# Eight-head mixer of a transformer kernel: values for two query tiles side by side with the values stationary, probabilities normalised on GpSimd, and no turn of the outputs

## The chip, the cores and the metric

One core of a Trainium2 chip runs the whole program. Its engines are TensorE (PE), VectorE (DVE), ScalarE (ACT), GpSimd (POOL) and SyncE (SP), each with its own instruction queue that it works off in order; they wait for each other by semaphores. The metric is the device time of one execution in microseconds, median of several runs.

## What is computed

Two transformer blocks, one after the other, on 512 tokens of width 1024, in float32. The stage that the change touches is the first half of the first block. It has two attention mixers over the same normalised input: an indexed one (called A1 in the kernel), whose keys for each query are the 128 with the best index score, and a latent one (B1) with eight heads of 64 and causal attention. In the latent mixer, per head and per block of 128 queries:

```
sc = (q_nope . k_nope + q_rope . k_rope) * scale
sc = where(causal, sc, -inf)
p  = softmax(sc)
o  = p @ v            # 128 queries x 64, for each of eight heads
...
y_b = o_b @ w_branch_b          # 512 -> 1024
merged = sigmoid(g_a) * y_a + sigmoid(g_b) * y_b
```

In the index part each of four query tiles needs its 128 largest of 512 scores. The kernel takes them in 16 rounds of eight.

## The kernel before

Every dense product is made of three matmuls per 128x128 weight tile: weights and inputs are split into a high and a low half (`w_hi`, `w_lo`, and the same for the inputs), and high times high, high times low and low times high are added up. ScalarE writes `w_hi` (L1710) and VectorE writes `w_lo` (L2272) for each set of weights, into one of two slots; TensorE may start an item when the first half of its tiles is split, and the split for the item after next comes when the item is done.

The stage is written out by hand as one list, `FRONT_ORDER`, which all engines walk, each doing its own part of each entry. `work_of_front` makes it. A unit is one head and one query tile: units 0 to 31 are the latent mixer (head u//4, tile u%4), units 32 to 63 the indexed one. For each unit v a slot of entries is laid down by `slot(v)`:

- `turn v+1`: TensorE transposes the 128x512 probabilities of unit v+1 (L1286), ScalarE copies them to `pt` (L1790), and then does the exponentials (L1781) that were asked for since the last turn;
- `score v+4`: TensorE makes the scores (L1250), VectorE adds the mask and takes the maximum (L2354 to L2360);
- `value v`: TensorE multiplies the turned probabilities with the values (L1296), ScalarE scales the result by one over the row sum and writes it to `front_rows` (L1801);
- `top`: one or two rounds of the largest-eight search, on VectorE alone (L2259 and L2260; at the end of a tile also L2262, L2263 and L2257);
- at the end of every second head `oturn`: TensorE transposes the 512x128 outputs of two heads (L1329), ScalarE and VectorE write their high and low halves (L1817, L2376).

At the start of a head there is `vturn`, which transposes its values. Between these entries, in each place that the list marks `None`, tiles of dense work are spread evenly: per head the item `bkv` (1 tile), `bq` (2 tiles) and a gate (8 tiles), and for the last two heads 24 tiles of the indexed mixer's projections. After a `bq` comes `rope`: a matmul (L1237), a multiplication on GpSimd (L1115) and two additions on VectorE (L2340, L2344). The split of the next weights (`later`) is issued by ScalarE and VectorE at the next `turn`, `vturn`, `oturn`, `value` or `both`.

Units from 32 on already work as the change makes the others work: GpSimd normalises the probabilities of two units before they are turned (L1123), and one `both` makes the values of two units with the values stationary and the probabilities moving (L1309). ScalarE and VectorE write the high and low halves of the result straight from the accumulator (L1823, L2382). VectorE inverts the row sums (L2369) of units j+1 and j+2 at `turn j`, for odd j, and waits there for the exponentials of unit j+2. For units below 32 it inverts unit j at `turn j`.

After the list, the branch products, the output projection, the feed-forward layers and the second block follow, most of the time; the change does not touch them.

Of the kernel before, what the change touches and what calls it, by code (L numbers as in the profile page):

```python
# [23 lines left out]
P = 128  # L24
D = 1024
SEQ = 512
META = 16
T = META + SEQ
# [150 lines left out]
def work_of_front():  # L179
# [23 lines left out]
    def slot(v):  # L203

        if v >= 32:
            p, e = (v - 32) // 2, [("vturn", 9)] if v == 32 else []
            if v % 2:
                e += [("both", p), None] + ([("turn", v + 1), None] if v + 1 < FRONT_VALUES else [])
# [10 lines left out]
        e += [("value", v), None]  # L219
        if v % 8 == 7:  # L220
            e += [("oturn", v // 8), None]
# [101 lines left out]
def front_outputs(v):  # L323

    return v + 1 if v < 32 else 32 + (v - 32) // 2 + 1
# [211 lines left out]
def events(phase):  # L537
# [5 lines left out]
    if kind == "front":  # L543
        e = items(len(FRONT_ITEMS[0::2]), len(FRONT_ITEMS[1::2]))
        units, ropes = FRONT_VALUES, len(ROPES)
        e.update(s_full=48, scored=units, negm=units, probs=units, rinv=units, o_full=48, o_out=48,
                 o_hi=16, normal=32, pt_full=len(FRONT_TURNED), pt_a=len(FRONT_TURNED), o_low=4, turned=ropes, roped=ropes, rope_step=ropes,
# [101 lines left out]
def build(nc, A, out):  # L649
    with ExitStack() as ctx:  # L650
# [226 lines left out]
        def front_output(k):  # L877

            return [x[:, k, META:T] for x in outputs["B1"]], turned_of

        def front_pair(p):

            i, t, _ = front_unit(32 + 2 * p)
            at, o = META + P * (t - 1), P * (1 + p % 2)
            return [x[:, i, at:at + P] for x in outputs["A1"]], acc[:, 3, o:o + P]
# [177 lines left out]
        def _(pool):  # L1063
# [10 lines left out]
            for index, ph in enumerate(PHASES):  # L1074
# [29 lines left out]
                if ph == ("front",):  # L1104

                    for what, j, *part in FRONT_ORDER:
# [13 lines left out]
                        elif what == "turn" and j >= 31 and j % 2 and j + 2 < FRONT_VALUES:  # L1120
                            for u in (j + 1, j + 2):
# [31 lines left out]
        def _(pe):  # L1153
# [39 lines left out]
            def front():  # L1193

                def dense(j, first, end):
# [3 lines left out]
                    if first == 0:  # L1199
# [4 lines left out]
                        if kind == "branch":  # L1204
                            if name == "B1":
                                pe.wait_ge(S["o_low"], n.at("o_low", 4))
                            else:
                                pe.wait_ge(S["o_out"], n.at("o_out", 48))
# [57 lines left out]
                def bank_free(x):  # L1266
# [4 lines left out]
                    else:  # L1271
                        pe.wait_ge(S["pt_a"], n.at("pt_a", x - 1))
                        kind, k = FRONT_TURN_LIST[x - 2]
                        if kind == "oturn":
                            pe.wait_ge(S["o_low"], n.at("o_low", k + 1))

                def turn_probs(v):

                    x = FRONT_TURNED["turn", v]
                    if v < 32:  # L1280
                        pe.wait_ge(S["probs"], n.at("probs", v + 1))
                    else:
                        pe.wait_ge(S["normal"], n.at("normal", v - 31))
# [6 lines left out]
                def values(v):  # L1290

                    made = FRONT_TURNED["vturn", front_unit(v)[0]]
                    pe.wait_ge(S["pt_a"], n.at("pt_a", max(FRONT_TURNED["turn", v], made) + 1))
                    pe.wait_ge(S["o_out"], n.at("o_out", v))
                    for b in range(4):
                        mm = pe.matmul(acc[:, 3, 64 * (v % 2):64 * (v % 2) + 64], pt[:, v % 2, 1 + b, :],  # L1296
                                       front_values(v)[:, 1 + b, 0:64], start=b == 0, stop=b == 3)
                    mm.then_inc(S["o_full"], 1)

                def values_of_pair(p):  # L1300

                    u = 32 + 2 * p
                    made = FRONT_TURNED["vturn", 8 + front_unit(u)[0] // 2]
                    pe.wait_ge(S["pt_a"], n.at("pt_a", max(FRONT_TURNED["turn", u + 1], made) + 1))
                    pe.wait_ge(S["o_out"], n.at("o_out", 32 + p))
# [7 lines left out]
                def turn_values(k):  # L1313
# [7 lines left out]
                    mm.then_inc(S["pt_full"], 1)  # L1321

                def turn_outputs(k):

                    pe.wait_ge(S["o_out"], n.at("o_out", 8 * k + 8))
                    x = FRONT_TURNED["oturn", k]
                    bank_free(x)
                    for b in range(4):
                        mm = pe.transpose(turned_of[x % 2][:, b * P:(b + 1) * P], front_rows[:, b, :], eye)  # L1329
                    mm.then_inc(S["pt_full"], 1)  # L1330
# [84 lines left out]
                for what, j, *part in FRONT_ORDER:  # L1415
# [24 lines left out]
                    elif what == "value":  # L1440
                        values(j)
                    elif what == "both":
                        values_of_pair(j)
                    elif what == "vturn":
                        turn_values(j)
                    elif what == "oturn":
                        turn_outputs(j)
# [254 lines left out]
        def _(act):  # L1702
# [30 lines left out]
            def front(following):  # L1733
# [59 lines left out]
                def take_output(v):  # L1793

                    at, t, _ = front_unit(v)
                    row, d = t - 1, 64 * (at % 2)
                    act.wait_ge(S["o_full"], n.at("o_full", v + 1))
                    act.wait_ge(S["rinv"], n.at("rinv", v + 1))
                    if v % 8 == 0 and v:
                        act.wait_ge(S["pt_full"], n.at("pt_full", FRONT_TURNED["oturn", v // 8 - 1] + 1))  # L1800
                    act.activation(front_rows[:, row, d:d + 64], acc[:, 3, 64 * (v % 2):64 * (v % 2) + 64], ACT.Identity,  # L1801
                                   scale=rinv8[:, v % 8:v % 8 + 1]).then_inc(S["o_out"], 1)

# [8 lines left out]
                def take_outputs(k):  # L1812

                    x = FRONT_TURNED["oturn", k]
                    (hi, _), bank = front_output(k)
                    act.wait_ge(S["pt_full"], n.at("pt_full", x + 1))
                    act.activation(hi, bank[x % 2], ACT.Copy).then_inc(S["pt_a"], 1)  # L1817
# [77 lines left out]
                for what, j, *part in FRONT_ORDER:  # L1895
# [41 lines left out]
                    elif what == "value":  # L1937
                        take_output(j)
# [4 lines left out]
                    elif what == "oturn":  # L1943
                        take_outputs(j)
# [265 lines left out]
        def _(dve):  # L2210
# [96 lines left out]
            def front(following):  # L2307
# [54 lines left out]
                def invert(v):  # L2362

                    dve.wait_ge(S["probs"], n.at("probs", v + 1))
                    if v >= 40:
                        dve.wait_ge(S["normal"], n.at("normal", v - 39))
                    elif v >= 8:
                        dve.wait_ge(S["o_out"], n.at("o_out", v - 7))
                    dve.reciprocal(rinv8[:, v % 8:v % 8 + 1], rowsum8[:, v % 8:v % 8 + 1]).then_inc(S["rinv"], 1)  # L2369

                def take_low(k):

                    x = FRONT_TURNED["oturn", k]
                    (hi, lo), bank = front_output(k)
                    dve.wait_ge(S["pt_a"], n.at("pt_a", x + 1))
                    dve.tensor_tensor(lo, bank[x % 2], hi.bitcast(F32), ALU.subtract).then_inc(S["o_low"], 1)  # L2376

                def take_both(p):

                    (hi, lo), bank = front_pair(p)  # L2380
                    dve.wait_ge(S["o_hi"], n.at("o_hi", p + 1))
                    dve.tensor_tensor(lo, bank, hi.bitcast(F32), ALU.subtract).then_inc(S["o_out"], 1)  # L2382
# [101 lines left out]
                for what, j, *part in FRONT_ORDER:  # L2484
# [420 lines left out]
```

## Time and profile before

| | |
|---|---|
| median of 3 runs | 2276.22 us (2275.92 to 2276.91) |
| the profiled execution | 2279.35 us, span 2277.5 us |
| granted TensorE clock, mean | 0.995 |
| TensorE busy | 2219.2 us (97%) |
| VectorE busy | 1243.9 us (55%) |
| ScalarE busy | 903.5 us (40%) |
| GpSimd busy | 220.5 us (10%) |
| eight heads of the latent mixer | about 130 to 300 us |

Busy time is that of recorded instructions; matmuls overlap each other in the records, so that TensorE can show as busy in a stretch in which it had short waits.

### The profile page before, as it was taken

The numbers are of one execution on the slowest core, as the hardware profiler recorded it, in microseconds if no ns is written. First come the engines' busy times: TensorE is split into PE (matmuls) and PEld (weight loads), VectorE is DVE, ScalarE is ACT, GpSimd is POOL, SyncE is SP. The second block draws the span as 40 slices with busy tenths as digits, with TensorE's granted clock in tenths as the row PEclk, the third lists the DMA queues.
The fourth block names the chain that finished last, engine by engine and source line by source line (L and its number), as shares of the span: only waits on it lengthen the run. The fifth ranks groups of instructions, "written<-read, shape, count | busy, mean of one in ns | idle before, by whom it ended". The sixth has DMA issues, their size and how long they took to land.

```text
span 2277.5 us, 36049 instructions
## 1 busy us (share of the span) xinstructions
PE 2219.2 (97%) x12592; PEld 1820.2 (80%) x12592; DVE 1243.9 (55%) x2668; ACT 903.5 (40%) x1815; POOL 220.5 (10%) x201
## 2 busy tenths in 40 slices
PE   8999999999999999999999899999999999999998
PEld 6567766778888889999999777777777787888887
DVE  5779786467736745533442545544555655443442
ACT  5455445444414443322322444444444433322332
POOL 0100043310000031000001000111100130000001
PEclk9999999999999999999999999999999999999999
DMA  4111211235533342342233222243333233332332
GB/s 119 36 37 37 65 47 52 79 102 150 157 102 95 113 129 78 91 129 88 85 106 99 57 85 81 74 111 94 98 92 98 81 97 89 95 108 77 97 105 75
DMA packets 400393, 205.67 MB, mean 90 GB/s; under 512 B 68956, under 2 KB 393928, under 8 KB 400284
## 3 DMA queue, kind: packets, MB, share of 16 engines
q1 hardware_dynamic: 399365, 203.83, 31.3%
q8 instruction: 63, 1.03, 0.2%
q10 hardware_dynamic: 919, 0.43, 0.1%
q14 instruction: 46, 0.38, 0.1%
HBM read 201.94 MB, written 14.80 MB: 95 GB/s over the span
## 4 chain that ended last, share of the span: by engine, by line
PE 64%; issue 19%; DVE 4%; ACT 2%; POOL 1%; POOLq 0%; DVEq 0%; ACTq 0%
PE acc L1169 34%; PE acc L1474 16%; PE acc L1220 5%; PE sco L1509 2%; PE acc L1573 1%; PE acc L1569 1%; DVE w_lo L2272 1%; PE sco L1262 1%; PE sco L1549 1%; POOL vT L1095 1%; PE acc L1309 1%; PE acc L1549 0%; PE sco L1529 0%; PE acc L1296 0%; DVE bias L2260 0%
## 5 line engine op out<-in xcount | busy, mean ns | idle before, releaser
L1710 ACT ACTIVATE w_hi<-raw 128x512 fp32r<-128x512 f32 (+4 forms) x656 | 372.0, 614 | 694.4 <-PE acc L1169 661.2
L2272 DVE TENSOR_TENSOR w_lo<-raw,w_hi 128x512 fp32r<-128x512 f32 (+4 forms) x656 | 423.2, 685 | 143.8 <-ACT w_hi L1710 139.5
L1169 PE MATMUL acc<-xn_hi,w_hi 128*128 128x512 f32 (+1 forms) x1408 | 421.1, 340 | 2.1 <-DVE qbuf L2826 2.1
L1169 PE MATMUL acc<-xn_lo,w_hi 128*128 128x512 f32 (+1 forms) x1408 | 422.1, 340 | 0.0
L1169 PE MATMUL acc<-xn_hi,w_lo 128*128 128x512 f32 (+1 forms) x1408 | 420.3, 339 | 0.0
L1169 PEld LDWEIGHTS acc<-xn_hi,w_hi 128*128 128x128 f32 x1408 | 241.9, 188 | 35.8 <-DVE qbuf L2826 3.0
L1169 PEld LDWEIGHTS acc<-xn_lo,w_hi 128*128 128x128 f32 x1408 | 241.2, 188 | 31.2 <-issue 0.5
L1169 PEld LDWEIGHTS acc<-xn_hi,w_lo 128*128 128x128 f32 x1408 | 241.5, 188 | 30.0
L1169 PE MATMUL acc<-hid_lo,w_hi 128*128 128x512 f32 (+1 forms) x832 | 261.5, 349 | 0.0
L1169 PE MATMUL acc<-hid_hi,w_lo 128*128 128x512 f32 (+1 forms) x832 | 260.6, 348 | 0.0
L1169 PE MATMUL acc<-hid_hi,w_hi 128*128 128x512 f32 (+1 forms) x832 | 259.8, 347 | 0.8 <-DVE hid_lo L2768 0.8
L2826 DVE TENSOR_TENSOR qbuf<-acc,v_tok 128x512 f32<-128x512 f32 (+1 forms) x132 | 91.7, 695 | 249.8 <-PE acc L1169 249.7
L1474 PE MATMUL acc<-xn_hi,w_hi 128*128 128x264 f32 (+1 forms) x576 | 187.7, 367 | 13.2 <-DVE xn_lo L2299 3.8
L2778 DVE SCALAR_TENSOR_TENSOR h<-acc,h 128x512 f32 (+3 forms) x64 | 44.5, 695 | 267.6 <-PE acc L1169 267.6
L1474 PE MATMUL acc<-xn_hi,w_lo 128*128 128x264 f32 (+1 forms) x576 | 172.8, 341 | 0.0
L1474 PE MATMUL acc<-xn_lo,w_hi 128*128 128x264 f32 (+1 forms) x576 | 172.5, 340 | 0.0
L1169 PEld LDWEIGHTS acc<-hid_hi,w_hi 128*128 128x128 f32 x832 | 144.5, 188 | 23.2 <-issue 1.1
L1169 PEld LDWEIGHTS acc<-hid_lo,w_hi 128*128 128x128 f32 x832 | 144.5, 188 | 21.2
L1169 PEld LDWEIGHTS acc<-hid_hi,w_lo 128*128 128x128 f32 x832 | 144.8, 188 | 20.4
L1474 PEld LDWEIGHTS acc<-xn_hi,w_hi 128*128 128x128 f32 x576 | 98.7, 189 | 36.8 <-issue 17.8
L1220 PE MATMUL acc<-xn_hi,w_hi 128*128 128x512 f32 x240 | 118.6, 494 | 0.9 <-DVE w_lo L2272 0.6
L1474 PEld LDWEIGHTS acc<-xn_hi,w_lo 128*128 128x128 f32 x576 | 99.3, 189 | 12.6
(397 smaller groups left out, 3065.7 us busy)
## 6 DMA issues: line engine op xcount, KB each, us to landing
raw<-in_w_ffn_in SPq DMA_DIRECT2D x176, 256.0 KB, 3.0
raw<-in_w_in SPq DMA_DIRECT2D x118, 256.0 KB, 3.2
raw<-in_w_up SPq DMA_DIRECT2D x88, 256.0 KB, 3.0
raw<-in_w_ffn_out SPq DMA_DIRECT2D x32, 384.0 KB, 3.3
raw<-in_w_gate SPq DMA_DIRECT2D x48, 256.0 KB, 3.0
raw<-in_w_ffn_out SPq DMA_DIRECT2D x32, 320.0 KB, 3.7
raw<-in_w_out SPq DMA_DIRECT2D x32, 256.0 KB, 2.8
bias<-grids_dram SPq DMA_DIRECT2D x64, 128.0 KB, 2.9
```

The lines of the kernel that those rows point to most:

```text
L1095: ins = pool.tensor_tensor(square_sum[:, c0:T], square_sum[:, c0:T], probs[:, s, c0:T], ALU.add)
L1169: mm = pe.matmul(acc[0:m, 2 * slot + b, 0:size], w[slot][:, t, 0:m], x[:, place(t), c:c + size], start=(t == 0 and w is w_hi and x is xh), ...
L1220: mm = pe.matmul(acc[0:m, slot, 0:SEQ], w[slot][:, t, 0:m], x[:, t, META:T], start=(t == 0 and w is w_hi and x is xh), stop=(t == tiles - ...
L1262: mm = pe.matmul(sco[:, hh, :], queries_a[i][r, P * (t - 1):P * t], kbuf[r, i // 2, META:T], start=True, stop=True)
L1309: mm = pe.matmul(acc[64 * hh:64 * hh + 64, 3, o:o + P], front_values(u)[:, 1 + b, 0:64], pt[:, hh, 1 + b, :], start=b == 0, stop=b == 3)
L1474: mm = pe.matmul(acc[:, b if wide else slot, 0:size], w[slot][:, t, :], x[:, t, c:c + size], start=(t == 0 and w is w_hi and x is xh), sto ...
L1509: mm = pe.matmul(sco[:, bank, to:to + size], qbuf[r, i % 2, TILES[t][0]:TILES[t][0] + P], kbuf[r, keys_at(name, i), c:c + size], start=Tru ...
L1549: mm = pe.transpose(turned_of[x % 2][:, b * P:(b + 1) * P], prob_of[u % 4][:, real + b * P:real + (b + 1) * P], eye)
L1710: act.activation(w_hi[slot][:, a:b, :], raw[slot][:, a:b, :], ACT.Copy).then_inc(S[f"hi_ready{slot}"], parts)
L2272: dve.tensor_tensor(w_lo[slot][:, a:b, :], raw[slot][:, a:b, :], w_hi[slot][:, a:b, :].bitcast(F32), ALU.subtract).then_inc(S[f"split{slot ...
L2778: dve.scalar_tensor_tensor(out=x, in0=banks(acc, 2 * s, blk), scalar=factor, in1=x, op0=ALU.mult, op1=ALU.add).then_inc(S[f"acc_free{s}"], 1)
L2826: dve.tensor_tensor(span(scaled[s], blk), banks(acc, 2 * s, blk), span(rstd, blk), ALU.mult).then_inc(S[f"acc_free{s}"], 1)
```

## The change

For units 0 to 31 `value` is replaced by `both`, once for two query tiles of the same head: the head's values (64 columns) are stationary and the turned probabilities move, tile t to rows 0 to 63 of the accumulator and tile t+1 to rows 64 to 127. The result is already turned, so the four `oturn` fall away. Because the row sum is then no longer on the rows of the result, the probabilities are normalised on GpSimd before they are turned, as for the units above 31, and `turn v` waits for that. ScalarE and VectorE write the output's halves with two instructions of 64x128 for each `both`. VectorE's inversions move: units 0 and 1 at `score 2` and `score 3`, all others in twos at the odd `turn`. With fewer entries a head has 10 places for dense tiles instead of 12 or 13.

```diff
         e = [("vturn", v // 4 + 1)] if v % 4 == 0 else []
-        if v + 1 < FRONT_VALUES:
-            e += [("turn", v + 1), None]
+        if v % 2:
+            e += [("both", v // 2), None]
+        e += [("turn", v + 1), None]
         if v + 4 < 32:
             e += [("score", v + 4), None]
         elif v >= 28 and v % 2 == 0 and (v - 28) // 2 < 16:
             e += [("pair", (v - 28) // 2), None]
-        e += [("value", v), None]
-        if v % 8 == 7:
-            e += [("oturn", v // 8), None]
...
-                        elif what == "turn" and j >= 31 and j % 2 and j + 2 < FRONT_VALUES:
-                            for u in (j + 1, j + 2):
+                        elif (what == "turn" and j % 2 and j + 2 < FRONT_VALUES) or (what == "score" and j == 3):
+                            for u in ((j + 1, j + 2) if what == "turn" else (0, 1)):
                                 pool.wait_ge(S["rinv"], n.at("rinv", u + 1))
                                 pool.tensor_scalar(front_probs[u % 4], front_probs[u % 4], rinv8[:, u % 8:u % 8 + 1], None,
                                                    ALU.mult).then_inc(S["normal"], 1)
...
                 def turn_probs(v):
 
                     x = FRONT_TURNED["turn", v]
-                    if v < 32:
-                        pe.wait_ge(S["probs"], n.at("probs", v + 1))
-                    else:
-                        pe.wait_ge(S["normal"], n.at("normal", v - 31))
+                    pe.wait_ge(S["normal"], n.at("normal", v + 1))
                     bank_free(x)
...
                 def take_both(p):
 
-                    (hi, _), bank = front_pair(p)
-                    act.wait_ge(S["o_full"], n.at("o_full", 32 + p + 1))
-                    act.activation(hi, bank, ACT.Copy).then_inc(S["o_hi"], 1)
+                    act.wait_ge(S["o_full"], n.at("o_full", p + 1))
+                    for (hi, _), bank in front_pair(p):
+                        last = act.activation(hi, bank, ACT.Copy)
+                    last.then_inc(S["o_hi"], 1)
...
                     elif what == "score":
                         score(j)
+                        if j in (2, 3):
+                            invert(j - 2)
...
                     elif what == "turn":
-                        if j < 32:
-                            invert(j)
-                        if j >= 31 and j % 2 and j + 2 < FRONT_VALUES:
+                        if j % 2 and j + 2 < FRONT_VALUES:
                             invert(j + 1)
                             invert(j + 2)
```

## Rows read from the trace of the kernel before

**Rows 1.** Busy time by engine: heads 0 to 5, heads 6 and 7, after them

```profile
core 0: us, PE busy (x) PEld busy (x) DVE busy (x) ACT busy (x) POOL busy (x), PEclk, DMA share, GB/s
132.05:245.68 113.63, 110.13 (x582) 80.77 (x583) 98.54 (x276) 64.65 (x156) 7.66 (x6) 1.00 0.18 45
245.68:301.63 55.95, 55.95 (x279) 42.09 (x279) 41.38 (x103) 25.89 (x59) 9.55 (x7) 1.00 0.20 50
301.63:341.00 39.37, 38.05 (x227) 25.07 (x226) 33.80 (x103) 17.51 (x44) 17.64 (x11) 1.00 0.18 51
```

**Rows 2.** Chain that ended last, in head 4: start, us, engine and line

```profile
212.88 0.86 PE sco L1250 x2
213.73 0.70 PE acc L1220 x3
215.29 0.84 PE acc L1296 x8
216.13 0.76 PE acc L1220 x3
216.89 0.44 PE sco L1286 x4
```

**Rows 3.** The same chain where values are already made in pairs

```profile
331.91 1.02 PE acc L1309 x16
332.93 0.89 PE acc L1220 x3
```

**Rows 4.** Timeline of head 4, VectorE and the turns of TensorE

```profile
207.48 0.63 PE L1286 MATMUL sco<-const,probs 128*128 128x128 f32 x4 [0.43 <-DVE hid_lo L2376]
210.68 0.15 DVE L2369 RECIPROCAL stats<-stats 128x1 f32<-128x1 f32 x1
214.60 0.14 DVE L2354 COPY small<-small 1x1 f32<-1x1 f32 x1
215.51 0.69 DVE L2340 TENSOR_TENSOR qbuf<-sco,aux 96x512 f32<-96x512 f32 x1
216.72 0.60 PE L1286 MATMUL sco<-const,aux 128*128 128x128 f32 x4
218.55 0.69 DVE L2259 MAX8 small<-bias 128x8 f32<-128x512 f32 x1
220.07 0.16 DVE L2369 RECIPROCAL stats<-stats 128x1 f32<-128x1 f32 x1
```

**Rows 5.** Timeline of VectorE at a later pair, with both halves' writes and a split

```profile
333.62 0.29 DVE L2382 TENSOR_TENSOR hid_lo<-acc,hid_hi 128x128 fp32r<-128x128 f32 x1
333.83 1.28 DVE L2272 TENSOR_TENSOR w_lo<-raw,w_hi 128x512 fp32r<-128x512 f32 x2
335.06 0.69 DVE L2318 SCALAR_TENSOR_TENSOR merged<-merged,acc 128x512 f32<-128x512 f32 x1
```

**Rows 6.** Timeline, GpSimd's normalisations and VectorE's splits beside them

```profile
305.67 0.20 DVE L2369 RECIPROCAL stats<-stats 128x1 f32<-128x1 f32 x2
305.91 3.10 POOL L1123 TENSOR_SCALAR aux<-aux,stats 128x512 f32<-128x512 f32 x2 [9.57 <-DVE stats L2369]
...
322.90 1.99 POOL L1123 TENSOR_SCALAR aux<-aux,stats 128x512 f32<-128x512 f32 x1 [3.86 <-DVE stats L2369]
...
361.68 1.72 DVE L2272 TENSOR_TENSOR w_lo<-raw,w_hi 128x512 fp32r<-128x512 f32 x2 [1.32 <-ACT w_hi L1710]
```

**Rows 7.** ScalarE's write of one pair's outputs, the line's instructions

```profile
L1823 ACT ACTIVATE hid_hi<-acc x16: 277/277/278, 307.6 to 422.1; 128x128 fp32r<-128x128 f32 x16
```

**Rows 8.** Timeline before the first head

```profile
127.95 1.02 PE L1250 MATMUL sco<-kbuf,qbuf 96*128 96x512 f32 x2
129.01 0.14 DVE L2354 COPY small<-small 1x1 f32<-1x1 f32 x1 [0.79 <-PE sco L1250]
129.87 0.15 DVE L2369 RECIPROCAL stats<-stats 128x1 f32<-128x1 f32 x1
130.20 0.60 PE L1286 MATMUL sco<-const,probs 128*128 128x128 f32 x4
132.05 0.63 PE L1286 MATMUL sco<-const,probs 128*128 128x128 f32 x4
```

More of the change, by code:

```diff
@@ L207, in slot @@
             if v % 2:
-                e += [("both", p), None] + ([("turn", v + 1), None] if v + 1 < FRONT_VALUES else [])
+                e += [("both", 16 + p), None] + ([("turn", v + 1), None] if v + 1 < FRONT_VALUES else [])
             else:
@@ L875, in front_values @@
             return values_of[at % 2 if u < 32 else at // 2]
-        def front_output(k):
-            return [x[:, k, META:T] for x in outputs["B1"]], turned_of
         def front_pair(p):
-            i, t, _ = front_unit(32 + 2 * p)
-            at, o = META + P * (t - 1), P * (1 + p % 2)
-            return [x[:, i, at:at + P] for x in outputs["A1"]], acc[:, 3, o:o + P]
+            o = P * (1 + p % 2)
+            if p >= 16:
+                i, t, _ = front_unit(2 * p)
+                return [([x[:, i, META + P * (t - 1):META + P * t] for x in outputs["A1"]], acc[:, 3, o:o + P])]
+            at, t, _ = front_unit(2 * p)
+            d = 64 * (at % 2)
+            return [([x[d:d + 64, at // 2, META + P * (t - 1 + hh):META + P * (t + hh)] for x in outputs["B1"]],
+                     acc[64 * hh:64 * hh + 64, 3, o:o + P]) for hh in range(2)]
         block = ctx.enter_context(nc.Block())
@@ L1288, in turn_probs @@
                     mm.then_inc(S["pt_full"], 1)
[L1290 to L1298, printed above, removed]
                 def values_of_pair(p):
-                    u = 32 + 2 * p
-                    made = FRONT_TURNED["vturn", 8 + front_unit(u)[0] // 2]
+                    u = 2 * p
+                    at, _, _ = front_unit(u)
+                    made = FRONT_TURNED["vturn", at if u < 32 else 8 + at // 2]
                     pe.wait_ge(S["pt_a"], n.at("pt_a", max(FRONT_TURNED["turn", u + 1], made) + 1))
-                    pe.wait_ge(S["o_out"], n.at("o_out", 32 + p))
+                    pe.wait_ge(S["o_out"], n.at("o_out", p))
                     o = P * (1 + p % 2)
@@ L1320, in turn_values @@
                                           eye[0:64, 0:64])
[L1321 to L1329, printed above, removed]
                     mm.then_inc(S["pt_full"], 1)
@@ L1439, in front @@
                         turn_probs(j)
-                    elif what == "value":
-                        values(j)
                     elif what == "both":
@@ L1445, in front @@
                         turn_values(j)
-                    elif what == "oturn":
-                        turn_outputs(j)
             def mixers():
@@ L2364, in invert @@
                     dve.wait_ge(S["probs"], n.at("probs", v + 1))
[L2365 to L2368, printed above, removed]
+                    if v >= 8:
+                        dve.wait_ge(S["normal"], n.at("normal", v - 7))
                     dve.reciprocal(rinv8[:, v % 8:v % 8 + 1], rowsum8[:, v % 8:v % 8 + 1]).then_inc(S["rinv"], 1)
[L2371 to L2376, printed above, removed]
                 def take_both(p):
-                    (hi, lo), bank = front_pair(p)
                     dve.wait_ge(S["o_hi"], n.at("o_hi", p + 1))
-                    dve.tensor_tensor(lo, bank, hi.bitcast(F32), ALU.subtract).then_inc(S["o_out"], 1)
+                    for (hi, lo), bank in front_pair(p):
+                        last = dve.tensor_tensor(lo, bank, hi.bitcast(F32), ALU.subtract)
+                    last.then_inc(S["o_out"], 1)
                 def first_split(j):
@@ L2541, in front @@
                         take_both(j)
-                    elif what == "oturn":
-                        take_low(j)
                     elif what == "top":
```

32 lines of the change are left out of this document (4 added, 28 removed).

## Prediction

> **What bounds the kernel now.** I read the page first (TensorE busy 97% of the span), then the windows of the stage that the change touches, then the chain of work that ended last through it, and last the timeline of VectorE against the turns of TensorE. The windows are cut at `turn 1`, `turn 25` and `turn 33`, so that the first holds heads 0 to 5 and the second heads 6 and 7. In both TensorE is busy nearly throughout. But VectorE is busy 98.5 of 113.6 us in heads 0 to 5, and only 41.4 of 56.0 in the next two, where there are 24 dense tiles a head instead of 11 [rows 1]. So in the first six heads two engines are near their limit, and what TensorE saves can be used only as far as VectorE follows. The chain there is mostly TensorE's [rows 2]. VectorE runs behind: it reaches its part of `turn 17` 3.2 us and that of `turn 19` 3.35 us after TensorE has started that turn [rows 4]. Now nothing hangs on that lag, since the turn waits only for exponentials done long before.
>
> **TensorE's work.** From the chain: a dense tile 0.70, a score 0.86 (the rope matmul has the same size, the same 0.86), a turn 0.44, a value 0.84 with 0.06 more in the tile behind it [rows 2]. A pair by `both` costs 1.02 and 0.19 more in the tile behind it, 1.21 [rows 3]. So two values, 1.80, become 1.21. An `oturn` is four transposes as a turn is: 0.44.
> A head of the first six after: 11 tiles 7.70, 4 scores 3.44, 4 turns 1.76, `vturn` 0.40, rope 0.86, 2 pairs 2.42: 16.6 us. Six are 99.6, with the longer turn behind a `vturn` some 100.3, against 113.6 now: at most 13.3 us could be saved. Heads 6 and 7 lose 8 values (7.2) and one `oturn` (0.44) and get 4 pairs (4.84): 2.8 us. VectorE has slack there, so I count that as gained.
>
> **The other engines.** ScalarE: 32 scalings go and 32 writes of 64x128 come; a 128x128 one takes 0.28 [rows 7]. It is busy 57% and the balance is near nothing. VectorE: 32 writes of low halves, 0.21 each from start to next start [rows 5], 6.7 us, less four of 128x512 (0.61 each, half of the 1.23 that the two in rows 5 take), 2.4: +4.3 us, most of it in the engine that has the least room. GpSimd: 32 normalisations at 1.55, 50 us [rows 6], which lie beside the rest but are now a link between VectorE and `turn`.
>
> **The first turns.** After `score 2` VectorE is done at 129.87 [rows 8], which is also when it inverts unit 0. GpSimd starts 0.24 after the inversion and takes 1.55 [rows 6]: `turn 0` at 131.7 instead of 130.20. `score 3` is then started at 132.1, VectorE takes it 1.06 later (129.01 against 127.95, [rows 8]), needs 0.91 (214.60 to 215.51, [rows 4]), and inverts unit 1 only then, since the inversion stands behind `score 3` in its queue; 1.8 for GpSimd: `turn 1` at 135.9 against 132.05. Cost 3.85 us, covered by nothing.
>
> **A head in steady state.** Let D be the time at which VectorE reaches its part of an odd turn. `turn j+1` can start at D + 0.24 + 1.55 + 0.05 = D + 1.85. TensorE's own way from `turn j` to `turn j+1` is turn 0.44, three tiles 2.10, score 0.86, pair 1.21: 4.6 us. With a lag over 2.75 TensorE waits; the lag now is 3.2 to 3.35 [rows 4]. It would only shrink if VectorE had room, so I walk one head.
> *From `turn 4h+1`.* VectorE: inversions 0.15, score 0.91, one search round 1.51 (218.55 to 220.07, [rows 4]), two low halves 0.42, D + 3.0. Only then comes the split of the gate's weights: in the list before, `value` stood between `bkv` and the round and issued it; now the next entry that issues it is `both`, behind the round. First half 0.61 [rows 5]: D + 3.6, and TensorE can't start the gate before 3.65 (its own way would bring it there at about D + 2.4). One tile, and rope starts at 4.35; VectorE rotates from 5.4, having been idle for 1.05 us, until 6.75 (two of 0.69, [rows 4]); score 0.91, two rounds 3.02: the next odd turn at D + 10.7, with TensorE 3.85 ahead.
> *From `turn 4h+3`.* VectorE's own 3.0 again, but the score it wants next stands behind `turn 4h+4`, which waits for GpSimd until 1.85; +0.44 +0.70 +1.06: 4.05. Score 0.91, two rounds 3.02, split of `bq` 0.36: 8.35, with TensorE 2.7 ahead.
> A head takes 10.7 + 8.35 = 19.05 us, with 2.1 of VectorE idle in it, and it closes on itself. The first head, which begins without lag, comes out at 18.4 by the same steps. The end of a search tile (masks, in heads 2 and 5) adds 2.8 in all. Six heads: 18.4 + 5 x 19.05 + 2.8 = 116.4 us, 2.8 more than now, instead of the 13.3 less that TensorE's work would allow.
>
> **GpSimd beside VectorE.** The gate's split now falls into the second normalisation of the pair (D + 1.8 to D + 3.35). Where a split started 0.1 us after a normalisation, two halves took 1.72 instead of 1.28, and where GpSimd started inside a split its instruction took 1.99 instead of 1.55 [rows 6]: 0.43 us a meeting. One a head on the path: 6 x 0.43 = 2.6 us.
> The Trainium skill, "SBUF — State Buffer", section "Who interferes with whom", says that a VectorE instruction with two SBUF inputs contends with a GpSimd instruction that reads SBUF, and in "SBUF: two separate sides" that the later one is blocked for the whole instruction. The trace agrees that they collide, but the delay it shows is 0.43 us and not the rest of the 1.55. By that rule the gate's first half would lose 0.35 us (3.0 to 3.35) and its second half up to 1.28 more to the rope multiplication, two thirds of it in VectorE's idle time; the six heads would then cost 4 us in place of 2.6.
>
> **Sum.** Start +3.85, heads 0 to 5 +2.8, collisions +2.6, heads 6 and 7 -2.8: +6.4 us. After `turn 33` the list is as before, and VectorE is there about 4 us behind TensorE either way, so nothing is gained or lost in the 39 us that follow, where VectorE is busy 33.8 [rows 1]. The profiled execution's 2279.35 becomes 2285.8; its execution lies 3.1 above the median of the runs, so for the median 2276.2 + 6.4 = 2282.6.
> Bounds: no collision on the path takes 2.6 off; each of VectorE's two idle times filled or stretched by 0.3 is 1.8 either way over six heads. The likeliest case's own range is 2280.8 to 2287.
>
> **Rivals.**
> *Faster.* The lag at odd turns falls below 2.75 us and the gate's split is in time, so that TensorE runs through. It needs VectorE to have 16.9 us of work a head (my two walks without idle) beside TensorE's 16.7, and no idle time. Then -13.3 -2.8 +3.85 = -12.3: 2264; half of it, 2270. For it: TensorE waits little now though VectorE is close. Against: both idle times follow from the order of the list, and 1.85 us of GpSimd has no cover. Chance 0.2, with all between 2264 and 2271.6.
> *No change.* The walk is right but the collisions stay in VectorE's idle time, and TensorE's lead at a head's end is worth a little: +3.8 or less, 2274 to 2280. Chance 0.3.
> *Much slower.* GpSimd becomes the link in a second place: the rope multiplication stands behind two normalisations (D + 3.35), in slot 29 right behind `turn 29`, and VectorE's rotation behind it. If each of the six heads waits for it as slot 29 will (until D + 4.65, and later still if `bq` is taken late), 1.3 us a head, 8 more: 2290. Against: in heads 0 to 5 the rotation is wanted at 5.4 anyway. Chance 0.1.
> *The forecast*, +6.4, has 0.4. A difference under 0.2% (4.6 us) can't be told from none.
>
> **How the numbers follow.** Slower by over 0.2% is the forecast and the much slower case, 0.5; within 0.2% is 0.3; faster 0.2. The range takes the no-change case whole and the faster one's nearer part on one side and reaches to 2290 on the other: 2269 to 2290.
>
> **What would show it.** In the profile after: `turn 0` 1.5 and `turn 1` near 3.9 us later; in heads 0 to 5 TensorE idle before L1286, released by GpSimd's normalisation, and before the gate's first tile, released by `w_lo`; six heads in 116 to 119 us with VectorE busy about 101; heads 6 and 7 in about 53. The prediction is wrong if six heads take under 110 us, which would mean that VectorE's lag had room to shrink, or if heads 6 and 7 don't gain.

## The result: slower, by nearly three times the forecast

The changed kernel takes 2294.22 us (median of 4 runs, 2293.36 to 2295.09), the kernel before 2276.26 beside it: ratio 1.0079, 95% interval 1.0067 to 1.0091, 18.0 us slower. The forecast was 2282.6, 6.4 us slower, with a range from 2269 to 2290. The sign was right, the size was not.

The windows of the changed kernel, cut at the same turns as [rows 1] (`turn 1`, 5, 9, 13, 17, 21, 25, 33):

```profile
core 0: us, PE busy (x) PEld busy (x) DVE busy (x) ACT busy (x) POOL busy (x), PEclk, DMA share, GB/s
134.76:156.12 21.36, 19.07 (x95) 12.35 (x96) 15.01 (x41) 8.77 (x21) 8.07 (x5) 0.91 0.12 30
156.12:176.14 20.02, 17.36 (x98) 11.12 (x96) 16.72 (x48) 10.33 (x26) 7.51 (x5) 1.00 0.13 35
176.14:196.03 19.89, 17.42 (x97) 11.12 (x95) 17.56 (x51) 10.20 (x26) 7.57 (x5) 1.00 0.14 35
196.03:216.95 20.92, 17.37 (x97) 11.12 (x96) 17.55 (x50) 10.34 (x26) 7.52 (x5) 1.00 0.13 34
216.95:236.85 19.90, 17.41 (x98) 11.12 (x96) 16.62 (x48) 10.21 (x26) 7.50 (x5) 1.00 0.15 36
236.85:262.65 25.80, 19.92 (x98) 12.81 (x96) 20.24 (x55) 11.19 (x27) 7.51 (x5) 0.87 0.25 62
262.65:316.63 53.98, 53.34 (x276) 37.63 (x274) 40.47 (x105) 25.80 (x59) 20.79 (x13) 1.00 0.18 46
```

Heads 0 to 5 take 127.89 us where they took 113.63: +14.3. In them TensorE is busy 108.5 us and idle 19.4; before it was idle 3.5. Heads 6 and 7 take 53.98 for 55.95: -2.0. From `turn 33` to `turn 63` nothing changed (117.92 us for 117.44). Ahead of the first head, from `score 2` to `turn 1`, it is 8.54 us (126.22 to 134.76) for 4.10 (127.95 to 132.05, [rows 8]): +4.4. These make +17.2 us. The two profiled executions as a whole differ by 14.1 (spans of 2277.5 and 2291.6): the profiled execution of the kernel before is itself 3.1 us above its median, and the changed one is 1.7 us shorter ahead of `score 2` and 1.4 shorter behind `turn 63`, where the change does nothing. (So turns are compared below by their distances and not by their times.)

What TensorE waits for between 126 and 300 us, by the waits:

```profile
engine line waited for: us in total, times, longest us
PE sco L1276 <- POOL probs L1122: 11.2, 5, 4.5
PE acc L1216 <- DVE w_lo L2219: 9.2, 12, 1.5
PE acc L1276 <- POOL probs L1122: 3.4, 3, 1.2
```

L1276 is the turn, L1216 a dense tile. So there are two kinds: 14.6 us for the normalisation, in 8 turns, and 9.2 us for low halves of weights. Both were in the forecast's list of signs. In the kernel before, the second kind is 0.8 us:

```profile
PE acc L1220 <- DVE w_lo L2272: 0.8, 3, 0.3
```

The timeline around the first turns:

```profile
126.22 1.02 PE L1246 MATMUL sco<-kbuf,qbuf 96*128 96x512 f32 x2
128.13 0.15 DVE L2314 RECIPROCAL stats<-stats 128x1 f32<-128x1 f32 x1
128.38 1.57 POOL L1122 TENSOR_SCALAR probs<-probs,stats 128x512 f32<-128x512 f32 x1 [12.40 <-DVE stats L2314]
...
130.00 0.66 PE L1276 MATMUL sco<-const,probs 128*128 128x128 f32 x4 [1.37 <-POOL probs L1122]
130.50 1.02 PE L1246 MATMUL sco<-kbuf,qbuf 96*128 96x512 f32 x2
...
132.89 0.21 DVE L2314 RECIPROCAL stats<-stats 128x1 f32<-128x1 f32 x2
133.14 1.56 POOL L1122 TENSOR_SCALAR probs<-probs,stats 128x512 f32<-128x512 f32 x1 [3.19 <-DVE stats L2314]
```

This is the chain that the prediction worked out: inversion, 0.25 us later GpSimd, 1.57 us, and `turn 0` 0.05 us behind it, then `score 3` behind `turn 0`, and unit 1's inversion behind `score 3`. What it did not have is the next window, of 134.76 to 138.00, right behind the 2.85 us wait of `turn 1`, and one behind the 4.45 us wait of `turn 24`. The column that reads 0.50 is the granted clock:

```profile
134.76:138.00 3.24, 3.24 (x10) 2.43 (x10) 0.00 (x0) 1.40 (x3) 3.03 (x2) 0.50 0.00 0
...
256.20:259.00 2.80, 2.80 (x8) 2.20 (x9) 1.19 (x3) 1.30 (x3) 1.45 (x1) 0.50 0.04 9
```

The granted clock is 0.50 there, the 1.2 GHz level: `turn 1` and `turn 24` each take 1.11 us instead of 0.66. It is 0.50 from 131.9, where the wait of `turn 1` begins, to 138.8, and from 254.7, inside the wait of `turn 24`, to 261.8. And why `turn 24` waits so long, in the timeline of ScalarE and VectorE before it:

```profile
244.44 0.71 ACT L1749 ACTIVATE probs<-probs,stats 128x512 f32<-128x512 f32 x1
...
249.30 0.68 DVE L2206 MAX8 small<-bias 128x8 f32<-128x512 f32 x1
...
250.80 0.43 DVE L2209 TENSOR_SCALAR bias<-bias 128x512 f32<-128x512 f32 x1
251.26 0.69 DVE L2210 TENSOR_TENSOR bias<-bias 128x512 f32<-128x512 f32 x1
251.99 0.14 DVE L2211 COPY small<-small 1x1 f32<-1x1 f32 x1
252.06 0.67 DVE L2204 TENSOR_TENSOR bias<-bias 128x512 f32<-128x512 f32 x1
252.76 0.69 DVE L2206 MAX8 small<-bias 128x8 f32<-128x512 f32 x1
...
254.28 0.24 DVE L2314 RECIPROCAL stats<-stats 128x1 f32<-128x1 f32 x2
```

L1749 is unit 24's exponential, done at 245.2. Its inversion comes 9 us later: it is made together with unit 25's, and stands behind a search round, the masks of a finished search tile (L2209 to L2211), the start of the next tile and another round, 5 us of work of which `turn 24` needs nothing.

### The profile page after: what moved, and what is told of

It is laid out like the page before. It is cut to its first block, busy times and chain, and to the rows that moved or that the text cites. A ratio compares the mean times of both kernels' runs of the same rounds, so it can differ in the third digit from the quotient of the medians.

```text
span 2291.6 us, 36031 instructions
## 1 busy us (share of the span) xinstructions
PE 2209.8 (96%) x12576; PEld 1799.3 (79%) x12576; DVE 1249.5 (55%) x2696; ACT 901.1 (39%) x1811; POOL 273.1 (12%) x233
## 4 chain that ended last, share of the span: by engine, by line
PE 62%; issue 19%; DVE 5%; ACT 2%; POOL 1%; POOLq 0%; DVEq 0%; ACTq 0%
PE acc L1168 34%; PE acc L1442 15%; PE acc L1216 4%; PE sco L1477 2%; PE acc L1541 1%; DVE w_lo L2219 1%; PE acc L1537 1%; PE acc L1290 1%; PE sco L1517 1%; POOL vT L1094 1%; DVE bias L2207 1%; PE sco L1258 1%; PE acc L1517 1%; DVE small L2206 0%; PE sco L1497 0%
## 5 line engine op out<-in xcount | busy, mean ns | idle before, releaser
L1216 PE MATMUL acc<-xn_hi,w_hi 128*128 128x512 f32 x240 | 119.1, 496 | 5.9 <-DVE w_lo L2219 5.7
```

What stands on the lines that cost most here:

```text
L1216: mm = pe.matmul(acc[0:m, slot, 0:SEQ], w[slot][:, t, 0:m], x[:, t, META:T], start=(t == 0 and w is w_hi and x is xh), stop=(t == tiles - ...
```

## The experiments

The kernel before, run beside them, had medians of 2276.39, 2276.13, 2275.97, 2276.84 and 2277.16 in the five groups of runs; the ratios are to these. Since these medians differ by up to 1.2 us, so may differences between runs of different groups.

**What the wait for the normalisation costs.** No normalisation, and no wait for it, in units 0 to 31; values still in pairs. The kernel leaves out the division by the row sum.

```
-                    pe.wait_ge(S["normal"], n.at("normal", v + 1))
+                    if v < 32:
+                        pe.wait_ge(S["probs"], n.at("probs", v + 1))
+                    else:
+                        pe.wait_ge(S["normal"], n.at("normal", v - 31))
```

> The changed kernel, but GpSimd does not normalise units 0 to 31 and their turns wait for the exponentials alone, as before the change; the division by the row sum is left out for the latent mixer. Theory A (a closed loop: VectorE's rounds, the late split of the gate's weights and the wait for the normalisation each hold TensorE in turn): the stalls before turns 0, 1, 24 and the odd-to-even ones go, the waits for w_lo stay; 2274 to 2280. Rival B (the wait for GpSimd is the whole loss): all of TensorE's saving appears, 2262 to 2266. Rival C (VectorE's load alone, whoever waits for it): no gain over the change, 2290 or more.

Measured: 2276.99, ratio 1.0000 (0.9990 to 1.0009), as theory A had it. So the normalisation, with its waits, costs 17 us, nearly all of the loss. But the matmuls saved by the pairs gave nothing: its waits show why.

```profile
engine line waited for: us in total, times, longest us
PE acc L1216 <- DVE w_lo L2222: 10.8, 11, 2.9
```

**The reverse: the kernel before with the normalisation alone**, values one unit at a time as before, ScalarE's scaling gone (`scale=rinv8[...]` out of the output's write).

> The kernel before with the normalisation alone: probabilities of units 0 to 31 normalised on GpSimd before their turn, inversions placed as in the change, values made one unit at a time as before, outputs copied without the scale. Theory A: the start's 4.4 + 1.9 us and 0.5 to 0.9 us at each of 11 even turns, 2288 to 2294, so that the normalisation's place accounts for nearly all of the loss. If the pairing of values is what costs: below 2280.

Measured: 2300.97, ratio 1.0112 (1.0095 to 1.0128), +24.8 us, 7 us more than theory A's range allowed. Its turns wait 17 us for GpSimd, up to 4.6 at `turn 24`, and its granted clock falls three times, where the changed kernel's falls twice. The pairs are therefore worth some 7 us in the presence of the waits (24.8 against 18.0).

**VectorE's other work.** The search rounds of tiles 0 and 1 left out, in the changed kernel and in the kernel before (`elif what == "top" and (j >= 2 or part[0] == TOPK // 8 - 1)`).

> The changed kernel without the search rounds of the first two query tiles (rounds 0 to 31, some 48 us of VectorE in slots 0 to 21; the masks at their end stay, what they select is not the reference's). Compared with the next run, the kernel before with the same left out. Theory A and rival C (VectorE is what TensorE's saving runs into): the change is now 8 to 12 us faster than the kernel before, since only the start's 4.4 us are left against 13.3 + 2. Rival B (GpSimd's link costs by itself): the change is still not faster.

> The kernel before without the search rounds of the first two query tiles. It waits little for VectorE as it is: 2269 to 2274, that is 2 to 7 us below the kernel before, by all theories.

Measured: 2280.85 (ratio 1.0021, 1.0012 to 1.0031), and 2276.20 (1.0003, 0.9993 to 1.0012). Both expectations missed: the kernel before became no faster without the rounds, where 2 to 7 us were expected, and the changed kernel stays 4.65 us slower than it, as rival B had it, where theory A had it 8 to 12 faster. Still, the same rounds cost the old kernel nothing and the changed one 13.4 us. Heads 1 to 4 take 17.5 to 17.6 us without them. But `turn 0`, `turn 1` and `turn 24` still wait 1.4, 2.8 and 3.7 us, so VectorE's load in rounds is not the cause of those (for `turn 24` the masks and the starts of the tiles were left in).

**The clock.** Idle matmuls before `turn 1` and `turn 24`, first 20 and 30, then 8 and 12 of them:

```
+                    if v in FILL:
+                        pe.wait_ge(S["roped"], n.at("roped", FILL[v][0]))
+                        for _ in range(FILL[v][1]):
+                            pe.matmul(sco[:, 2, 0:P], ones[:, :], eye, start=True, stop=True)
```

> The changed kernel with idle matmuls (ones times the identity, into the rope bank, results unused) in front of turn 1 (20 of them) and turn 24 (30), where TensorE waited 2.85 and 4.45 us and the granted clock then fell from 2.4 to 1.2 GHz for some 4 to 5 us each. If the low clock behind these two waits costs time by itself: 4 us less than the change, 2289 to 2291, with a granted clock of 1.00 in heads 0 and 5. If not (VectorE sets the pace there anyway): 2294, no change.

> The changed kernel with idle matmuls on TensorE in front of turn 1 (8 of them) and turn 24 (12), fewer than in the run with 20 and 30, which overshot the wait by 3.5 us at turn 1. Theory A (the fall of the granted clock after the two long waits costs about 1.9 and 2.6 us, and the waits themselves are not lengthened by so few matmuls): 2289.5 to 2291.5, turn 1 at its old distance from turn 0 and the step from turn 1 to 2 at 4.6 us for 6.5. Rival (what the two stretches lose is the work that piled up, and not the clock): 2293.5 to 2294.5.

Measured: 2293.40 with 20 and 30, where the filler itself pushed `turn 1` back by 3.3 us and `turn 24` by 2.1; 2290.67 with 8 and 12 (ratio 1.0063, 1.0051 to 1.0076), in the middle of what was expected. The turns of the latter:

```profile
134.69 0.66 PE L1281 MATMUL sco<-const,probs 128*128 128x128 f32 x4 [0.86 <-POOL probs L1123]
...
139.33 0.60 PE L1281 MATMUL acc<-const,aux 128*128 128x128 f32 x4
...
254.26 0.66 PE L1281 MATMUL sco<-const,probs 128*128 128x128 f32 x4 [1.77 <-POOL probs L1123]
...
258.19 0.66 PE L1281 MATMUL sco<-const,probs 128*128 128x128 f32 x4
```

`turn 1` starts as late as before (4.75 us behind `turn 0`, and 4.76 in the changed kernel), but `turn 2` follows in 4.64 us instead of 6.52, and `turn 25` behind `turn 24` in 3.93 instead of 6.49. The same work at 2.4 GHz: the two falls cost 1.9 and 2.6 us in the profiled execution. The medians differ by less, 3.5 us (2294.22 against 2290.67).

The run with 20 and 30 shows that the long wait is not needed for a fall. There the idle matmuls began at 132.04 and TensorE was busy from 130.21 on; its only wait since 126 was the 1.37 us of `turn 0`. Still the clock fell, to 0.50 for most of this window:

```profile
132.00:135.60 3.60, 3.60 (x19) 3.56 (x18) 1.44 (x8) 1.08 (x3) 2.26 (x2) 0.53 0.08 18
```

**Inversions earlier.** First only those of units 0 and 1, at `score 1` and `score 2` in place of `score 2` and `score 3`; then also the even units' (a unit's inversion right behind the next score, ahead of the rounds), each normalised as it is inverted:

```
+                        if j in (1, 2):
+                            invert(j - 1)
+                        elif j % 2:
+                            invert(j - 1)
```

> The changed kernel with the inversions of units 0 and 1 one entry earlier (at score 1 and score 2) and their normalisation at score 2. If the start's cost is the wait plus the low clock behind it: turn 1 about 3.5 us earlier, head 0 about 2 us shorter, 2288 to 2290. If the low clock comes from elsewhere: 2290.5 to 2291.

> The run before, and the inversion and normalisation of each even unit moved in front of the two search rounds (to the odd score) instead of behind them. Theory A: the waits of TensorE for GpSimd at turns 4, 8, 12, 16, 20 and 24 go; what is left are the waits for w_lo, as in the run without normalisation: 2274 to 2280. Rival B' (GpSimd's time itself, beside VectorE, is what costs): no more than 2 us below the run before.

Measured: 2289.21 (ratio 1.0055, 1.0038 to 1.0072), as expected, and 2280.65 (1.0020, 1.0010 to 1.0030), just above theory A's range. With both, the waits for GpSimd are down to one of 0.8 us, 13.6 us are won back in all, and the waits for low halves have grown to 13.0 us, 11 times.

**Who holds the low halves.** On top of it, the rounds of even slots moved behind the next pair (`("top", ...)` put behind `("both", v // 2)`):

> The run before, and each even slot's search round moved behind the next pair of values, so that the low halves and the split of the gate's weights come before it. Theory A: now nothing of the loop is left but ScalarE's order, and a good part of TensorE's saving of 13 + 2 us appears: 2264 to 2272. If the late split was not VectorE's round but the pair itself, behind which ScalarE splits: 2274 to 2278, no change from the run before.

Measured: 2283.82 (1.0029, 1.0019 to 1.0039), in neither range: 3.2 us above the run before it, with intervals that overlap, and in any case no gain. That theory falls, at least as the rounds' place beside the pair goes. The timeline of the changed kernel at a gate's split shows another holder ahead of VectorE:

```profile
180.99 0.56 ACT L1773 ACTIVATE hid_hi<-acc 64x128 fp32r<-64x128 f32 x2 [1.70 <-PE acc L1290]
...
181.45 1.14 ACT L1678 ACTIVATE w_hi<-raw 128x512 fp32r<-128x512 f32 x2
181.65 0.59 DVE L2320 TENSOR_TENSOR hid_lo<-acc,hid_hi 64x128 fp32r<-64x128 f32 x2 [0.35 <-ACT hid_hi L1773]
...
182.16 1.28 DVE L2219 TENSOR_TENSOR w_lo<-raw,w_hi 128x512 fp32r<-128x512 f32 x2
...
182.89 0.50 PE L1216 MATMUL acc<-xn_hi,w_hi 128*128 128x512 f32 x1 [0.64 <-DVE w_lo L2219]
```

ScalarE waits 1.70 us for the pair's outputs and only then makes the weights' high half, whose raw values had been there: both engines' loops issue the split behind `both`. So the split was put ahead of it, in both loops, first for `both` alone and then for more entries:

```
+                    if what in ("both", "score", "turn", "vturn", "top") and later is not None:
+                        split_item(later)
+                        later = None
```

The runs differ in this list and in the kernel that it is put into. `both` alone, in the changed kernel:

> The changed kernel, with ScalarE and VectorE splitting the weights of the item taken before they take a pair's outputs, not behind it. Theory A (in heads 0 to 5 the splits stand behind the pair on ScalarE, which makes the heads 19.9 to 20.0 us for the 19.05 forecast): the weights wait of about 0.6 us a pair goes, 2288 to 2291. Rival B (the outputs of the pair, or VectorE's own order, hold the weights as much): 2293 to 2295, the waits only change their place.

Measured: 2290.56 (1.0063, 1.0051 to 1.0075), 3.7 us won, and in the ordinary heads 1 to 4 (`turn 5` to `turn 21`) 3.3 of their 80.7 us:

```profile
156.56:233.98 77.42, 68.85 (x382) 44.49 (x380) 68.47 (x196) 40.94 (x101) 30.03 (x20) 1.00 0.15 37
```

`both` alone, with the early inversions:

> The kernel with the units' inversions and normalisations moved ahead (the one that took 2280.65 us), with the splits before the pair as well. That kernel still waited for low halves of the weights 12 times for 13.3 us together. Theory A (most of these are splits behind the pair): 2274 to 2277, at or under the kernel before. Rival B (they are VectorE's rounds and inversions, or the exps on ScalarE): 2279.5 to 2281.

Measured: 2278.49 (1.0010, 1.0001 to 1.0018), between the two theories: 2.2 us won, which is hardly clear of noise (1.0010 to 1.0030 without it). With `score`, `turn` and `vturn` too:

> As the run before it, with the splits also ahead of each turn, vturn and score on ScalarE and VectorE, so that no copy, exponential or search round stands ahead of a split whose weights are there. Theory A (every low half that is waited for is late by what its engine does ahead of it): 2270 to 2275. Rival B (the copies of the turned probabilities are now late in their place): 2277 to 2282.

Measured: 2276.70 (1.0002, 0.9992 to 1.0012). That is above what A gave and a little below B. It still waits 8.4 us for low halves, 5 times, with VectorE running two rounds ahead of a split. With `top` as well:

> The kernel with early inversions and splits ahead of the pair, turns and scores (2276.70 us), which still waits five times for low halves of the weights, 8.4 us together: at 187.8 and 148.9 us of its trace VectorE runs two search rounds with the weights' high half ready 4 us before. Here VectorE splits ahead of search rounds too. Theory A (the late low halves were behind the rounds alone): two waits of 2.6 and 2.95 us go, and with them the half clock behind each, 2267 to 2272, below the kernel before. Rival B (the rounds, pushed back, make the inversions or masks late, or GpSimd's operations now hold VectorE's): 2275 to 2279.

Measured: 2269.07 (0.9972, 0.9963 to 0.9981): 7.8 us under the kernel before. Theory A holds, and this is the version to keep. It still waits 3.1 us for low halves, in 6 small waits. Its windows for heads 0 to 5 and for 6 and 7:

```profile
129.26:147.24 17.98, 16.94 (x95) 11.07 (x95) 14.45 (x40) 9.74 (x24) 7.51 (x5) 1.00 0.16 39
147.24:164.44 17.20, 16.98 (x97) 11.20 (x95) 16.51 (x49) 10.54 (x26) 8.50 (x5) 1.00 0.15 41
164.44:181.79 17.35, 16.96 (x97) 11.26 (x96) 16.66 (x49) 10.60 (x26) 8.52 (x5) 1.00 0.17 41
181.79:200.94 19.15, 17.25 (x98) 11.12 (x96) 18.36 (x53) 10.59 (x26) 9.05 (x5) 1.00 0.15 38
200.94:218.30 17.36, 16.96 (x98) 11.24 (x96) 16.66 (x50) 10.59 (x26) 8.52 (x5) 1.00 0.16 41
218.30:237.71 19.41, 17.24 (x98) 11.21 (x96) 18.66 (x52) 11.00 (x27) 8.53 (x5) 1.00 0.33 81
237.71:291.47 53.76, 53.28 (x275) 37.63 (x275) 43.59 (x113) 25.71 (x60) 21.01 (x13) 1.00 0.21 55
```

Six heads in 108.45 us, for 113.63 before and 127.89 in the changed kernel; heads 6 and 7 in 53.76, for 53.98 in the changed kernel, so that nearly all of the gain is in the first six. The clock stays at 1.00. In the second, third and fifth head VectorE and TensorE are both busy 16.5 to 17.0 of 17.2 to 17.4 us: now two engines are nearly full. Only the fourth and the sixth head are longer, and those are the ones in which VectorE alone has 18.4 and 18.7 us of work.

**Controls.** The same split order in the kernel before, in the changed kernel without normalisation, and in the changed kernel as it is:

> The kernel before, with the same rule for splits (ahead of each turn, score, value, pair and search round) and nothing else. Theory A (the kernel before waits only 0.8 us for low halves in heads 0 to 7, so there is nothing to win): 2275 to 2277. Rival B (split order costs it as well, hidden in its other waits): under 2272, and what the order gives would then have nothing to do with the change.

> The changed kernel without the GpSimd normalisation and its wait for units 0 to 31 (the division is left out), with the splits ahead of everything: what pairing the values is worth by itself. Without the split order it took 2276.99. Theory A (its 12 waits for low halves, 11.1 us, ate what pairing saves): 2265 to 2269. Rival B (pairing itself saves next to nothing on TensorE): 2274 to 2277.

> The changed kernel with the full split order (ahead of pairs, turns, scores and search rounds) and with the inversions and normalisations where the change puts them. Theory A (the two faults add up: late normalisation costs what the early inversions gave back, some 13.6 us, and splits behind pairs and rounds cost the rest): 2283 to 2288, with about 15 us of waits for the normalisation left. Rival B (the split order alone mends most, since a unit normalised early is worth something only through it): under 2280.

Measured: 2279.11 (1.0013, 1.0004 to 1.0022), so the order is worth nothing to the kernel before, and rather costs it a little; 2267.80 (0.9964, 0.9950 to 0.9977), so the pairs give 9 us once the waits for low halves are small (4.6 us, for 10.8 in the run without normalisation above), and the normalisation, at the right place, costs 1.3 (2269.07 against 2267.80), which the spread of the two does not tell from nothing; and 2298.68 (1.0093, 1.0076 to 1.0109), which neither theory had. By itself the order makes the changed kernel 4.5 us slower, or 3.6 with each against the kernel before of its own group; the intervals of the ratios overlap, but the six heads in the trace are 3.5 us longer too (131.34 for 127.89). Its waits on TensorE and on VectorE (the latter between 126 and 245 us):

```profile
PE sco L1276 <- POOL probs L1122: 8.8, 5, 3.0
PE sco L1276 <- POOL aux L1122: 7.1, 3, 2.9
PE acc L1276 <- POOL aux L1122: 4.3, 2, 2.1
PE acc L1276 <- POOL probs L1122: 2.6, 3, 1.2
```

```profile
DVE w_lo L2222 <- ACT w_hi L1678: 12.8, 7, 4.4
```

Not one wait for a low half is left, and the turns wait 22.8 us for the normalisation instead of 14.6. VectorE now stands 12.8 us at splits for ScalarE's high half (9.0 in the changed kernel), and inversions queue behind them. And the split is now next in VectorE's queue behind an inversion, so that it starts 0.1 us before the normalisation that the inversion released:

```profile
223.33 1.27 DVE L2222 TENSOR_TENSOR w_lo<-raw,w_hi 128x512 fp32r<-128x512 f32 x2
223.43 4.06 POOL L1122 TENSOR_SCALAR aux<-aux,stats 128x512 f32<-128x512 f32 x2 [6.79 <-DVE stats L2317]
```

The pair of normalisations takes 4.06 us instead of 3.11. The same happens in five heads, ahead of turns 6, 10, 14, 18 and 22, and each of these turns waits 2.1 to 2.9 us where in the changed kernel it waits for nothing. How much of the loss is this meeting and how much the later inversion no run separates. The two repairs don't add: the early inversions alone give 13.6 us, the split order alone loses 3.6 to 4.5, both together give 25.2.

## Why the prediction was right in sign and wrong in size

**Start, +3.85: measured +4.4.** Right by the timeline above, but for one step: VectorE took up `score 3` 1.5 us after TensorE had begun it (130.50 to 132.04) and not 1.06, since a split of weights, waiting for ScalarE's high half, stood ahead of it until then.

**Heads 6 and 7, -2.8: measured -2.0**, and **nothing after `turn 33`: measured +0.5.** Right, within 0.8 and 0.5 us.

**Heads 0 to 5, +2.8, and collisions, +2.6: measured +14.3 together.** This is the step that failed, the sum 18.4 + 5 x 19.05 + 2.8 = 116.4 us, with the collisions 119.0, against 127.9. It had the right mechanism, with both waits at the places named, and four terms were mis-sized or missing; they make +4.5, +2.8, +4.2 and -2.6, the 8.9 us between the two:
- *The clock, 0 in the sum, measured 4.5.* The sum priced a wait at its length. At two of them the clock fell to 1.2 GHz, which cost 1.9 and 2.6 us more in the trace. In the trace with 8 and 12 idle matmuls both are gone; its median gave 3.5 back.
- *The sixth head, measured 25.8, of which 2.6 is the clock.* The walk gave it 19.05 and its half of the search tiles' ends. The rest is 2.8 us above the forecast. The timeline shows the masks ahead of an inversion, so that they delay `turn 24` by their whole length, and the item split in this slot is one of eight tiles and not of one; that these two make the 2.8 us is read from the timeline, no run takes them out.
- *The ordinary heads, 19.05 forecast.* Heads 1 to 4 take 80.7 us for some 77.6 by the forecast, head 0 takes 19.5 without the clock for 18.4: 4.2 us. The walk looked only for what stood ahead of the split on VectorE. The split is two instructions, and the high half on ScalarE stands behind the pair's write, which itself waits for TensorE. Putting the split ahead of the pair gave 3.7 us back, and with it heads 1 to 4 take the 77.4 us above.
- *Collisions, 2.6 forecast, none found on the path.* In heads 1 to 5 of the changed kernel the gate's splits take 1.28 us and pairs of normalisations 3.11 (once 3.19), as alone: the split starts only as the pair ends (in the third head at 182.16, the pair ending at 182.21). It is the late high half that keeps them apart, so this is luck and no property of the change. In the first head GpSimd's rope multiplication meets the split (1.94 us for 1.28) and the next split is slower too (0.73 for 0.29). The rule of the Trainium skill weighed there ("SBUF — State Buffer", "SBUF: two separate sides": the later instruction is blocked for the whole of the other) gets better support from the kernel with the split order alone, where the rope multiplication and a split do meet:

```profile
248.80 1.28 POOL L1114 TENSOR_TENSOR bias<-qbuf,aux 96x512 f32<-96x512 f32 x1
248.83 2.40 DVE L2222 TENSOR_TENSOR w_lo<-raw,w_hi 128x512 fp32r<-128x512 f32 x2
```

The split takes 2.40 us for 1.28, that is 1.12 more, nearly all of the 1.25 us that GpSimd's instruction still had to run. A `TENSOR_SCALAR`, one input, cost it 0.43 with 1.45 us still to run [rows 6]; this one has two inputs. The other way round the delay is long as well: the normalisation that starts 0.1 us inside a split of 1.27 us loses 0.95 (4.06 for 3.11). The 0.44 us of [rows 6], 1.99 for 1.55, was beside a split of only 0.74 us in all (322.80 in the trace of before), so that for this direction the prediction's price of 0.43 us a meeting was read from a short split. And the prediction's own sum by that rule is off: 0.35 and a third of 1.28 are 0.78 us a head, 4.7 for six heads and not 4.

**VectorE as the second bound.** Right, and the experiments bear it out: the search rounds cost 13.4 us in the changed kernel and none before. But the forecast took its 2.1 us of idle time a head as given. It came from the order of the list, and the faster rival's condition ("VectorE has 16.9 us of work a head beside TensorE's 16.7, and no idle time") is what the version to keep nearly meets in its second, third and fifth head: 16.5 to 16.7 beside 17.0, and 17.2 to 17.4 us a head. Its 2269.07 lies in what the rival forecast, 2264 to 2270, but for another kernel than the one that was forecast.

**The much slower rival**, at 2290, was near in number and wrong in cause: in heads 0 to 5 VectorE waits for GpSimd nowhere, so no rotation stood behind the normalisations.

Open stays why the part ahead of `score 2` differs by 2 us between executions, and what decides whether the clock falls at a wait, and for how long.

## What to carry to other kernels

When a step that was off the path (an inversion, a weights' split) becomes a link, look up what its queue holds ahead of it on every engine that has a half of it, and move it to the first point at which its inputs are there, all such steps together: here one repair alone gave 13.6 us, the other alone lost some 4, both gave 25.2. Price a long wait on TensorE at its length plus what the lower clock may cost behind it; here that was 1.9 us behind a wait of 2.85 and 2.6 behind one of 4.45, and less behind the same wait of `turn 24` in two other runs. And if an experiment removes the new wait and nothing is won, ask what the saved work ran into before giving up the change: the pairs were worth 9 us only after the second wait was cut to less than half.

## What the runs showed of the hardware

Waits of 1.2 us (turns 8, 12, 16 and 20) left the granted clock at 1.00 in the heads that hold them. In the changed kernel the waits of 2.85 and 4.45 us each went with a stretch at 0.50. But the length of the wait does not decide it alone. With 20 idle matmuls in place of the wait of `turn 1` the clock stood at 0.50 from 132.0 to 135.4 all the same, with TensorE busy since 130.21 behind a wait of 1.37 us. In the run with the split order alone `turn 14` waited 2.87 us, and the clock was 1.00 in that wait and in the windows before and behind it, while waits of 2.1 us in the same run were followed by 0.50. Nor is the price fixed: the step from `turn 24` to `turn 25` takes 3.93 us at 2.4 GHz, 6.49 in the changed kernel, but 5.57 and 5.29 behind waits of 4.46 and 4.52 us in the runs with the first inversions earlier and with the split ahead of `both`. With 8 and 12 idle matmuls (0.86 and 1.77 us of wait were left) the clock stayed at 1.00 throughout.

A VectorE split that starts inside a GpSimd `TENSOR_TENSOR` (two inputs) loses nearly what that still has to run: 1.12 of 1.25 us, 1.11 of 1.24, 0.75 of 0.88 in the run with the split order alone, 0.41 of 0.54 in the changed kernel. Inside a `TENSOR_SCALAR` (one input) it lost 0.43 of 1.45 [rows 6]. That the number of inputs makes the difference is argued, not shown. A GpSimd instruction that starts inside a split is delayed too: a `TENSOR_SCALAR` by 0.95 us of the 1.17 that the split still had to run.
